# Expert weights in slots of 512 KB, routing sums on VectorE, index scores between products

## What is computed

```python
def dsa_attention(q, k, v, iq, ik, iw):          # 16 heads, 8 index heads, top 64 keys
    ...
        logits = jnp.einsum('bqhd,bsd->bqhs', iqi, ik, preferred_element_type=jnp.float32)
        score = jnp.einsum('bqh,bqhs->bqs', iwi, jax.nn.relu(logits))
        score = jnp.where((kpos[None, :] <= qpos[:, None])[None], score, -jnp.inf)
        _, idx = lax.top_k(score, topk)
        ...

def moe_swiglu(h, router_w, router_b, w_gate, w_up, w_down):
    t = h.reshape(B * S, Dm)
    logits = (t @ router_w).astype(jnp.float32) + router_b.astype(jnp.float32)
    top_vals, top_idx = lax.top_k(logits, TOP_K)                 # 2 of 8 experts
    gates = jax.nn.softmax(top_vals, axis=-1)
    combine = jnp.sum(jax.nn.one_hot(top_idx, N_EXPERTS) * gates[..., None], axis=1)
    for e in range(N_EXPERTS):
        out = out + combine[:, e:e + 1] * swiglu(t, w_gate[e], w_up[e], w_down[e])
```

## Time and profile before

| | |
|---|---|
| median of 3 runs | 1308.31 us (1305.67 to 1310.41) |
| the profiled execution: its own time | 1310.03 us |
| its span, first to last instruction | 1308.4 us |
| PE busy | 1272.9 us (97%) |
| DVE, ACT, POOL busy | 646.3, 278.4, 77.4 us |
| granted TensorE clock, mean | 0.988 |
| DMA | 368.19 MB, mean 281 GB/s |

### The profile page before, as it was taken

How to read it: one execution, slowest core, us unless ns; L and a number is a source line. 1 busy time by engine, 2 the same in 40 slices (tenths; PEclk the granted TensorE clock), 3 DMA queues, 4 the chain that set the end, 5 groups by cost and what they waited for, 6 DMA issues and landing times.

```text
span 1308.4 us, 26922 instructions
## 1 busy us (share of the span) xinstructions
PE 1272.9 (97%) x10788; PEld 970.8 (74%) x10788; DVE 646.3 (49%) x1640; ACT 278.4 (21%) x730; POOL 77.4 (6%) x130
## 2 busy tenths in 40 slices
PE   6999999999999999999999999999999999999997
PEld 4768888999999767799999987778574565445545
DVE  5355555888887625457677766662631011001103
ACT  4332303112112414520000022164100000000002
POOL 0100000000000000000000001000110000000020
PEclk9999999999999999999999999899899999999998
DMA  9999783677776662236777772802999999999990
GB/s 352 413 400 406 294 287 113 225 278 266 269 283 237 248 221 81 93 118 257 278 269 272 280 299 81 354 1 97 388 404 405 409 417 406 408 413 417 407 376 33
DMA packets 73878, 368.19 MB, mean 281 GB/s; under 512 B 8243, under 2 KB 8499, under 8 KB 49034
## 3 DMA queue, kind: packets, MB, share of 16 engines
q1 hardware_dynamic: 56594, 271.28, 54.2%
q0 software_dynamic: 17216, 95.98, 19.1%
HBM read 347.16 MB, written 20.06 MB: 281 GB/s over the span
## 4 chain that ended last, share of the span: by engine, by line
PE 91%; DVE 3%; issue 2%; DMA 2%; ACT 2%; SPq 1%; POOL 0%; ACTq 0%; DVEq 0%; POOLq 0%
PE banks L955 20%; PE banks L686 17%; PE banks L942 11%; PE banks L1275 11%; PE banks L1322 8%; PE banks L1297 4%; PE banks L711 4%; PE banks L806 2%; PE banks L766 2%; PE banks L1022 2%; PE banks L871 1%; PE banks L855 1%; DMA ring<-stream 1%; PE banks L882 1%; DMA logit<-hrows 1%
## 5 line engine op out<-in xcount | busy, mean ns | idle before, releaser
L1275 PE MATMUL banks<-ring,arena 128*32 128x512 f32 x1536 | 169.0, 599 | 0.7 <-DVE arena L2190 0.7
L1714 DVE CUSTOM_DVE_ANT_0 side<-side 128x1024 f32<-128x1024 f32 x128 | 151.1, 1220 | 36.2 <-DMA side<-ada 36.1
L942 PE MATMUL banks<-arena,ring 128*128 128x256 f32 x704 | 160.2, 380 | 0.0
L2278 DVE TENSOR_TENSOR arena<-arena,banks 128x256 f32<-128x256 f32 (+1 forms) x48 | 15.1, 330 | 271.8 <-ACT arena L1651 271.8
L686 PE MATMUL banks<-h,ring 128*128 128x256 f32 x640 | 143.6, 382 | 0.9 <-ACT arena L1375 0.5
L942 PEld LDWEIGHTS banks<-arena,ring 128*128 128x128 f32 x704 | 130.2, 190 | 17.2 <-issue 1.4
L686 PEld LDWEIGHTS banks<-h,ring 128*128 128x128 f32 x640 | 120.0, 190 | 22.6 <-ACT arena L1375 3.7
L1275 PEld LDWEIGHTS banks<-ring,arena 128*32 128x32 f32 x1536 | 51.2, 111 | 113.3 <-issue 112.3
L686 PE MATMUL banks<-arena,ring 128*128 128x256 f32 x384 | 84.2, 380 | 0.5 <-ACT arena L1468 0.5
L955 PEld LDWEIGHTS banks<-h,ring 128*128 128x128 f32 x672 | 81.5, 192 | 2.1
L955 PE MATMUL banks<-arena 128*128 128x128 f32 x672 | 81.9, 275 | 0.0
(11 more groups left out here) (327 smaller groups left out, 1590.2 us busy)
## 6 DMA issues: line engine op xcount, KB each, us to landing
ring<-stream SPq DMA_DIRECT2D x247, 512.0 KB, 5.6
ring<-experts SPq DMA_DIRECT2D x96, 1024.0 KB, 21.7
side<-ada POOLq DMA_DIRECT2D x64, 1024.0 KB, 7.8
side<-experts SPq DMA_DIRECT2D x24, 1024.0 KB
arena<-experts SPq DMA_DIRECT2D x8, 1024.0 KB
yrows<-side POOLq DMA_DIRECT2D x1, 6144.0 KB, 32.1
hrows<-side POOLq DMA_DIRECT2D x1, 5632.0 KB, 18.1
arena<-lasts SPq DMA_DIRECT2D x8, 512.0 KB
```

What stands on the lines that cost most here:

```text
L942: last = pe.matmul(banks[:, 4 + c // 2, (c % 2) * T:(c % 2 + 1) * T], ring[:, s, c * P:(c + 1) * P], hid[:, j % 2, :], start=False, stop=F ...
L1275: ins = pe.matmul(banks[BLOCK * j:BLOCK * (j + 1), t, :], hg[:, k, BLOCK * t:BLOCK * (t + 1)], ring[:, m, (j % 2) * 512:(j % 2 + 1) * 512] ...
L1714: dve.tensor_tensor_reduce(weights, weights, cond[:, 0 if layer0 else 1, :], 1.0, 0.0, ALU.mult, ALU.add, accum_out=msum[:, n:n + 1]).then ...
```

## The change

1. **Single slots.** `experts` is laid out as one block of 512 KB for each slot, `lasts` is gone. SP issues 33 DMAs of 512 KB for each expert in place of 17, each waiting for its own slot; PE waits for each slot's own semaphore, in the same number of waits.
2. **Order of the first expert.** For expert 0 SP takes the slots in the order of their last reading by the stream before (7 to 19, the six of `side`, 20 to 23, 0 to 6, the three of `arena`).
3. **Row sums on DVE.** The two additions of `brow` go from POOL to DVE, behind the second half of the gathered tokens, and write to `hrow` (the place of `h`), from which the scatter now reads.
4. **Targets first.** The prefix sums of `slot_numbers` read a zeroed margin and need no copies (5 instructions for 10); `row_numbers` treats both token tiles in one instruction and ends with the scatter's row numbers; the shares (`row_shares`) and the tables (`tables`, which stood ahead of it all) come behind.
5. **Index scores between products.** The scores of heads 0 and 1 stand ahead of the rotation, those of heads 2 to 7 after each pair of chunks of `dv`.

```diff
+            def last_read(m):
+                if m >= RING:
+                    return U["dq", 4].pos if m < TAIL else total
+                return max(n + (total - 1 - n) // RING * RING for n in range(m, m + 1))
...
-            for m in range(0, MSLOTS, 2):
+            sides = 0
+            for m in sorted(range(MSLOTS), key=last_read):
                 if m < RING:
-                    sp.wait_ge(slot_used[m], before[m])
-                    sp.wait_ge(slot_used[m + 1], before[m + 1])
-                elif m == RING:
-                    sp.wait_ge(s_mod, 9)
-                    sp.wait_ge(nought_out, 64)
+                    for n in range(m, m + 1):
+                        sp.wait_ge(slot_used[n], before[n])
+                elif m < TAIL:
+                    if sides == 0:
+                        sp.wait_ge(s_mod, 9)
+                        sp.wait_ge(nought_out, 64)
+                    sides += 1
...
-                sp.dma_start(moe_pair(m), lasts[0] if m == MSLOTS - 1 else experts[m // 2]).then_inc(slot_full[m], 16)
+                sp.dma_start(moe_slot(m), experts[m]).then_inc(slot_full[m], 16)
             with sp.Fori(1, EXPERTS - 1) as p:
-                for m in range(0, MSLOTS, 2):
-                    sp.wait_ge(*emptied(min(m + 1, MSLOTS - 1), p))
-                    sp.dma_start(moe_pair(m), weights(m, p)).then_inc(slot_full[m], 16)
+                for m in range(MSLOTS):
+                    sp.wait_ge(*emptied(m, p))
+                    sp.dma_start(moe_slot(m), weights(m, p)).then_inc(slot_full[m], 16)
...
-            pool.wait_ge(s_gather, 2)
-            for tile in range(2):
-                rows = htok[:, tile, :].rearrange("t (c p) -> t c p", c=KC)
-                pool.tensor_tensor(rows, rows, brow.rearrange("t (p c) -> t c p", c=KC), ALU.add).then_inc(consts_set, 1)
-            pool.wait_ge(consts_set, 6)
+            pool.wait_ge(consts_set, 7)
             pool.wait_ge(s_routed, 1)
             for k in range(4):
                 pool.indirect_dma_start(hrows, bass.IndirectOffsetOnAxis(ap=target[:, k:k + 1], axis=0),
-                                        htok[:, k // 2, :], None).then_inc(rows_stored, 16)
+                                        hrow[:, k // 2, :], None).then_inc(rows_stored, 16)
...
+            index_scores(0)
+            index_scores(1)
             rotate(10, dkT[:, 0], taken(U["dk", 0]))
             u = U["dv"]
-            token_unit(u, 0, 2, T, 0, release=False)
-            token_unit(u, 1, 2, T, T, do_begin=False)
+            for n in range(8):
+                token_unit(u, n // 4, 2, T, (n // 4) * T, release=(n >= 4), do_begin=(n == 0), chunks=range(2 * (n % 4), 2 * (n % 4) + 2))
+                if n < 6:
+                    index_scores(2 + n)
...
-                                pe.wait_ge(slot_full[m - m % 2], 16 * (before[m - m % 2] + p + 1))
+                                pe.wait_ge(slot_full[m], 16 * (before[m] + p + 1))
...
             first_rows(1, s_hg_high)
-            link(dve.memset(tab, 0.0), s_route)
+            dve.wait_ge(s_h, 44)
+            dve.wait_ge(*U["htok", 3].done)
             for tile in range(2):
-                link(dve.tensor_copy(tab[:, 0:EXPERTS, tile], rank[:, tile, :]), s_route)
-                link(dve.tensor_copy(tab[:, 0:EXPERTS, 2 + tile], comb[:, tile, :]), s_route)
-            link(dve.tensor_copy(cur, tab[:, 0, :]), s_route)
+                dve.tensor_tensor(hrow[:, tile, :].rearrange("t (c p) -> t c p", c=KC), htok[:, tile, :].rearrange("t (c p) -> t c p", c=KC),
+                                  brow.rearrange("t (p c) -> t c p", c=KC), ALU.add).then_inc(consts_set, 1)
...
                 if first:
                     slot_numbers()
                     row_numbers()
+                    tables()
+                    row_shares()
                     extra_passes()
                     last_choice()
```

More of the change, by code:

```diff
@@ L219, in program @@
 def program(nc, xT, cols_d, mats_d, pos_d, table_d, sel_d, poolA_d, poolw_d, stream, cond_d, ada,
-            experts, lasts, out):
+            experts, out):
     ctx = ExitStack()
@@ L355, in program @@
         early, late = htok, h[:, :, :].rearrange("p (a c) n -> p a (c n)", a=2)
+        hrow = late
         slot_full = [sem(f"slot_full{s}") for s in range(MSLOTS)]
@@ L579, in _ @@
                 expert = sp.value_load(ints[0:1, bass.ds(p, 1)], min_val=0, max_val=EXPERTS - 1)
-                for m in range(0, MSLOTS, 2):
-                    sp.wait_ge(*emptied(min(m + 1, MSLOTS - 1), p))
-                    sp.dma_start(moe_pair(m), weights(m, expert)).then_inc(slot_full[m], 16)
+                for m in range(MSLOTS):
+                    sp.wait_ge(*emptied(m, p))
+                    sp.dma_start(moe_slot(m), weights(m, expert)).then_inc(slot_full[m], 16)
             for c in range(0, KC, 2):
@@ L700, in one, with token_unit @@
                 project(u, moving, r=r).then_inc(slot_used[u.pos % RING], 1)
-            def token_unit(u, tile, slots, width, at=0, release=True, do_begin=True):
+            def token_unit(u, tile, slots, width, at=0, release=True, do_begin=True, chunks=range(KC)):
                 if do_begin:
@@ L706, in token_unit @@
                 per = KC // slots
-                for kc in range(KC):
+                for kc in chunks:
                     s = (u.pos + kc // per) % RING
@@ L1158, in _, with index_scores @@
             rotate(9, iqT[:, 3], taken(U["iq", 3]))
-            for m in range(8):
+            def index_scores(m):
                 pe.wait_ge(s_rope, 7 + m // 2)
@@ L2192, in slot_numbers, with tables @@
             def slot_numbers():
[L2194 to L2200 removed]
+                at = OVER
+                for shift, to in ((1, SUM1), (2, SUM2), (4, SUM1), (8, SUM2)):
+                    link(dve.tensor_tensor(rt[:, to:to + 16], rt[:, at:at + 16], rt[:, at - shift:at - shift + 16], ALU.add), s_route)
+                    at = to
+                link(dve.tensor_tensor(slotno, rt[:, at:at + 16], over, ALU.mult), s_route)
+            def tables():
+                link(dve.memset(tab, 0.0), s_route)
+                for tile in range(2):
+                    link(dve.tensor_copy(tab[:, 0:EXPERTS, tile], rank[:, tile, :]), s_route)
+                    link(dve.tensor_copy(tab[:, 0:EXPERTS, 2 + tile], comb[:, tile, :]), s_route)
+                link(dve.tensor_copy(cur, tab[:, 0, :]), s_route)
             def extra_passes():
@@ L2221, in extra_passes, with both_tiles @@
                 dve.engine_nop().then_inc(s_routed, 1)
+            g1, d2, flags, rowno = rt[:, 244:252], rt[:, 252:260], two(260, 8), two(296, 8)
+            best, total, keep = rt[:, 276:280], rt[:, 280:282], rt[:, 284:288]
+            share, bound, both = rt[:, 288:292], rt[:, 292:293], rt[:, 188:196]
             def row_numbers():
-                base, g1, d2, flags, rowno = (rt[:, a:a + 8] for a in (236, 244, 252, 260, 268))
-                best, total, keep = rt[:, 276:280], rt[:, 280:282], rt[:, 284:288]
-                share, bound, both = rt[:, 288:292], rt[:, 292:293], rt[:, 296:304]
-                link(dve.tensor_scalar(base, mat("small", 0, 8), float(CAP), None, ALU.mult), s_route)
+                def both_tiles(v):
+                    return v.unsqueeze(1).broadcast_to([P, 2, EXPERTS])
+                first, second = (best.rearrange("p (a k) -> p k a", k=2)[:, k, :] for k in range(2))
                 link(dve.tensor_scalar(g1, slotno[:, 0:8], float(CAP), float((EXPERTS - 2) * CAP), ALU.mult, ALU.add), s_route)
@@ new lines, in row_numbers, with row_shares @@
+                link(dve.tensor_reduce(first, rowno, AX, ALU.max), s_route)
+                link(dve.tensor_reduce(total, rowno, AX, ALU.add), s_route)
+                link(dve.tensor_tensor(second, total, first, ALU.subtract), s_route)
+                link(dve.tensor_scalar(keep, best, 1.0, None, ALU.subtract), s_route)
+                link(dve.tensor_copy(target, keep), s_route)
+                dve.engine_nop().then_inc(s_routed, 1)
+            def row_shares():
+                link(dve.tensor_scalar(bound, rt[:, 480:481], float(CAP), float((EXPERTS - 1) * CAP), ALU.mult, ALU.add), s_route)
+                for k in range(4):
+                    tile = k // 2
+                    link(dve.scalar_tensor_tensor(both, rowno[:, tile, :], best[:, k:k + 1], comb[:, tile, :], ALU.is_equal, ALU.mult), s_route)
+                    link(dve.tensor_reduce(share[:, k:k + 1], both, AX, ALU.add), s_route)
```

58 lines of the change are left out of this document (19 added, 39 removed).

## The result

| | before | changed |
|---|---|---|
| median of 5 runs | 1306.0 us (1305.67 to 1310.41) | 1300.0 us (1298.37 to 1301.22) |
| ratio, 95% interval | | 0.9939 (0.992 to 0.9958) |
| span of the profiled execution | 1308.4 us | 1299.6 us |
| PE, DVE, POOL busy | 1272.9, 646.3, 77.4 us | 1268.5, 643.3, 71.6 us |

The change is 0.6% faster, at the time forecast: 1300.0 against 1300.4. A second run of it gave 1299.96 us beside 1309.27 for the kernel before, a ratio of 0.9932. Between the two profiled executions lie 8.8 us. The gain is not the one forecast: 7.9 us were counted off a median of three executions, 1308.3 us; over five that median is 1306.0, and the gain 6.0 us. The steps do not all hold.

The account below looks back on a forecast made before the run. The prediction took PE's chain of work to bound the expert passes, so the start of pass 1 counts. Gains of 3.5 + 1.9 + 2.5 = 7.9 us off 1308.3 gave 1300.4 us, range 1297.2 to 1305.0.

Parts of the forecast that it names:

- the three terms: Gains summed: index scores 3.5 us, wait before pass 1's row transposes 1.9, slow clock at pass 1 2.5; together 7.9.
- The wait at the row transposes: End of pass 0: a scatter starting 7.7 us earlier removes PE's wait for rows; gain 1.9 us.
- The slow clock at pass 1: Pass 1's wide part: with no gap before it, 23.11 us falls to 20.60; gain 2.5 us.
- The rival that it stays: Pass 1: the clock falls all the same, 2.5 us still paid; 1302.9 us, chance 20%.
- The index scores, 3.5 us: First score to first `dq` product: mixing scores with `dv` products covers relu waits, 18.1 us becomes 14.6.
- the work of the stretch at full clock and without waits: Index scores: 5.8 us for scores, 7.2 for `dv`, 0.9 for two rotations; together 13.9 us.
- a few short stalls: Pass 0: short PE stalls that an emptier queue might remove, worth 0 to 1.5 us; taken as 0.
- Order of the first expert, 0 us: First expert's loads set out near 790 us, taking backlog off the queue; 0 us by itself.
- the lag stays hidden: Expert passes: queue lag grows some 6 us more, but from about 6 us rather than 20, costing nothing.
- Single slots, 0 us: Expert passes: 512 KB loads need 43.2 us of transfer instead of 42.4, within a 43.6 us pass; 0 us.
- transfers bind the passes: Expert passes: transfers over 48.6 us a pass, below 372 GB/s, would decide; at 359 GB/s 1313 us, chance 5%.
- the things to look for: Expected profile signs: scores 14 to 15 us, earlier scatter and loads, no idle before pass 0's row transposes, passes of 43.6 us.

Follow-up runs that it names:

- the new routing: Kernel before with only the row sums moved to DVE and the scatter's targets computed first; 1301.59 us, ratio 0.9963.
- the second profile: The kernel before, unchanged, run and profiled again; median 1306.17 us, ratio 1.0012.
- twos: The change with its six mixed index scores in three groups of two neighbours: 1296.17 us with single slots, 1295.87 us with 1 MB slot pairs.
- pairs: The change with slots loaded two at a time (1 MB, 8 KB rows), new order of the first expert kept; 1298.65 us, ratio 0.994.

## Why the prediction was right, point by point

The time was right to 0.4 us, but that closely by luck: the gain was 6.0 us, 1.9 less than the 7.9 forecast, and the median of the kernel before, from which they were taken off, lay 2.3 us lower over five executions than over three. (The second run has 9.3 us, beside slower executions of the kernel before.) Two of the three terms stood, the third was too large, and one thing that was not in the sum came on top. With the sizes found below, 1.9 + 2.3 + 0.5 for the terms and 1.7 for that, the sum would have been 6.4 us.

*The wait at the row transposes, 1.9 us: right, by one of three ways.* The scatter moved as worked out (9.7 us behind the start of pass 0 for "some 9", the two sums 4.05 us for 4.0, which was the middle of two far bounds and so a lucky hit), and the new routing does it alone. So does the new order alone, and so do the single slots (no wait with old routing and old order). The prediction gave 0 to the latter two; each takes away the same wait of 2 us again, which is why together they give no more.

*The slow clock at pass 1, 2.5 us: right, 2.3 in the profiles.* The rival that it stays had 20%. In the three profiles with the wait (2 us of idle PE, then the transposes) 1.7 to 3.4 us are lost to the clock at the start of pass 1; in the eleven without it, none, though the 0.7 us of copying `hg` stay in all of them. So the wait of about 2 us costs about twice what the wait view says.

*The index scores, 3.5 us: the mechanism did not hold, and its size was off.* The step that failed is the work of the stretch at full clock and without waits, put at 13.9 us. It is 15.3, and with the wait for DVE 15.8, where 14.6 was forecast. The scores take 0.86 + 6 x 0.85 = 6.0 us, near the 5.8 of the sum; but the sum took single scores to be what scores are worth, where the row at its start, shows four instructions in 0.50 us and hence two scores at once. `dv` in groups takes 0.95 + 5 x 1.06 + 2.00 = 8.3 us for 7.2, the rotations 1.1 for 0.9, and the wait for DVE 0.5 for 0.7. And "before" was no fixed 18.1: the stretch took 14.8 us in the second profile. In the five profiles with the scores together it took 14.3, 14.8, 16.4, 17.7 and 18.1 us, a mean of 16.3; in the seven with them mixed singly 15.8 each. The mean gain is about half a microsecond, too little for the measurement of it alone to tell from none (0.999). I had read one execution's slow clock as a property of the order of the instructions. That mixing keeps the clock up is likely from the profiles (none of the seven, nor of the two in twos, lost any there, three of five did), but no run separates it from chance, and the cause of the fall isn't settled.

*What made up for it.* Pass 0 had a stall of its own of 1.7 us behind its 26th narrow product (`0.90 <-issue`, and slow products behind it), which is gone with the change; the prediction gave "a few short stalls" as 0 to 1.5 and took 0. Of the six profiles with the routing of before it is there in five (not in the change with the old routing), and in none of the eight with the new one. It is not PE's alone. In the kernel before, PE and ACT come back together, ACT with its first silu of the pass, whose products had ended by 952.8 us:

```profile
955.19 6.93 PE L1297 MATMUL banks<-ring,arena 128*32 128x192 f32 x163 [0.90 <-issue]
955.29 0.94 ACT L1651 ACTIVATE arena<-banks 128x256 f32<-128x256 f32 x3 [30.48 <-remote]
```

That silu starts 2.6 to 2.7 us behind the first narrow product in all five, and 0.3 us behind it in the nine profiles without the stall. What holds them stays open: no wait of the profile explains it. To compare like with like, I take the second profile of before and that of the change again, both with 5.1 us of slow clock at the three places: 1303.3 - 1298.4 = 4.9 us. Pass 0 gives 4.2 (wait and stall), pass 1 and after 2.7 (1.7 of it the clock at pass 1), the first score starts 0.6 earlier; the scores cost 1.0, and the stretch to the gather 1.6, its slow clock being 1.7 longer. The medians differ by more, 6.0 and 9.3 us in the two comparisons, along with the clock: the kernel before has executions down to 0.987, and the change had none below 0.992.

*Order of the first expert, 0 us: wrong as a number, right as a cover.* The prediction said that the lag stays hidden because it grows "from about 6 us rather than 20". It started at 12.3 and not at 6, and ended at 15.6; but take the new order away, and single slots run out of cover in the last pass: +7.8 us (1307.71 for 1299.96). The prediction had said what that would cost, and not that the new order is what pays for it. *Single slots, 0 us: right only beside the order.* Against pairs, they give nothing with the new order (1299.96 and 1298.65 us, ratios 0.9932 and 0.994; with twos 1296.17 and 1295.87), and with the old order they lose what the routing gains (1307.71, where pairs with the old order and the new routing have 1301.59, with their scores together, which took 0.6 us more in that profile). With all else in place they cost nothing and bring nothing but a quicker scatter, which is slack by then. The loss was the rival to which I gave 5%, "transfers bind the passes"; it was judged by the rate alone (400 against 372 GB/s), and the last pass was bound at 395, since the queue was late when pass 1 began (16.8 us behind its start) and lost 8.8 us more by pass 6. The Trainium skill's rule in the page "DMA: Bandwidth & Descriptors", section "Bandwidth", to batch to at least 1 MiB, points the right way in these runs: 408 GB/s of the queue's busy time with 1 MB and 395 with 512 KB, 3%, and it is worth 0 or 6 us according to the lag.

Of the things to look for, "14 to 15 us" for the scores was wrong (15.8); all others came true, the wide part of pass 1 with 20.81 us for 20.6. The new fall of the clock at 910 to 915 us costs 5.39 us for 16 products that took 3.7; it is in other variants as well (the routing alone, the order alone) and not in some with the same work, so I put it down to no part of the change.

## What to carry to other kernels

Price a stretch by its work at full clock and look at a second profile before counting a slow clock as gain: here 3.3 us of it came and went, while the slow clock behind a 2 us wait was there every time. When a transfer's form is made worse (smaller DMAs), ask how late the queue is when the bound stretch begins, not only whether the rate suffices; an earlier start may be all that pays for it. Three edits that each remove the same wait don't add up, and undoing one of them shows nothing (1299.85 us for 1299.96 without the new routing): put each alone on the kernel before as well (the new routing alone gives 4.7 us). And when instructions are spread out to cover waits, keep together those that run at the same time.

## What the runs showed of the hardware

- Two products over rows 0 to 63 and 64 to 127 that follow each other run at the same time: one score alone 0.85 us, two 0.86.
- The same 32 products of 128x256 take 7.1 us in a row, 7.7 in pieces with three pairs of scores among them, and 8.3 in pieces with six single ones, all at full clock.
- A POOL addition slows DVE's small copies that run beside it (2.31 us for one that takes 0.17 alone); the same two additions on DVE cost 4.05 us in all, less than POOL's 5.71.
- Two busy DMA queues take turns by packets and not by bytes (573 to 558, 385 to 381): smaller rows in the bulk queue give the other one more of the engines. The same scatter was waited for 11.1 to 16.4 us.
